# A state-space scan whose entering states are read into token rows and turned back by TensorE

## The reference

```
acum = jnp.cumsum(dtc * a_neg.reshape(ng, nr), axis=2)
decay = jnp.exp(jnp.where(mask, seg, -jnp.inf))
scores = jnp.einsum('bcign,bcjgn->bcijg', cc, bc)
y_intra = jnp.einsum('bcijgr,bcjgrp->bcigrp', scores[..., None] * decay, xdt)
...
y_inter = jnp.einsum('bcign,bcgrpn,bcigr->bcigrp', cc, s_prev, jnp.exp(acum))
y = (y_intra + y_inter)
```

## Time and profile before

| | us |
|---|---|
| median of 3 runs | 1627.63 |
| lowest and highest run | 1621.13, 1632.57 |
| span of the profiled execution | 1621.1 |
| TensorE busy in it | 1537.1 (95%) |
| DVE, ACT, POOL busy | 869.4, 795.1, 904.1 |

### The profile page before, as it was taken

How to read it: one execution, slowest core, us unless ns; L and a number is a source line. 1 busy time by engine, 2 the same in 40 slices (tenths; PEclk the granted TensorE clock), 3 DMA queues, 4 the chain that set the end, 5 groups by cost and what they waited for, 6 DMA issues and landing times.

```text
span 1621.1 us, 30898 instructions
## 1 busy us (share of the span) xinstructions
PE 1537.1 (95%) x11703; PEld 1460.5 (90%) x11703; DVE 869.4 (54%) x1806; ACT 795.1 (49%) x1450; POOL 904.1 (56%) x516
## 2 busy tenths in 40 slices
PE   4999998999999999999999999999989999999996
PEld 2899997887898999999899989789788989999996
DVE  0633202777436777712573449498873247777423
ACT  1655435767335544423676564565553345444333
POOL 0455555677572555557255556777753634555552
PEclk9999999999999999999999999999979999999998
DMA  8334346887551434434134323101213423344430
GB/s 334 103 117 127 121 129 215 289 302 264 188 163 53 125 121 129 145 130 155 52 93 157 105 92 104 41 27 41 40 52 133 143 91 105 129 130 128 136 125 39
DMA packets 57729, 209.63 MB, mean 129 GB/s; under 512 B 6288, under 2 KB 6416, under 8 KB 57232
## 3 DMA queue, kind: packets, MB, share of 16 engines
q1 hardware_dynamic: 56464, 205.96, 39.0%
q10 hardware_dynamic: 1152, 2.10, 0.4%
HBM read 200.63 MB, written 7.41 MB: 128 GB/s over the span
## 4 chain that ended last, share of the span: by engine, by line
PE 74%; issue 10%; DVE 8%; POOL 4%; ACT 3%; DMA 1%; POOLq 0%; DVEq 0%; SPq 0%; ACTq 0%
PE ps L755 6%; PE ps L757 6%; PE ps L756 6%; PE ps L663 6%; PE ps L665 6%; PE ps L664 6%; PE ps L998 4%; PE ps L999 4%; PE ps L1000 4%; PE ps L2737 3%; PE ps L2739 3%; PE ps L2738 3%; POOL wlo L318 3%; PE ps L388 2%; DVE ps L2311 2%
## 5 line engine op out<-in xcount | busy, mean ns | idle before, releaser
L318 POOL TENSOR_TENSOR wlo<-raw,whi 128x1024 fp32r<-128x1024 f32 (+1 forms) x195 | 494.1, 2535 | 445.7 <-ACT whi L306 445.4
L306 ACT ACTIVATE whi<-raw 128x1024 fp32r<-128x1024 f32 (+1 forms) x241 | 265.6, 1103 | 517.9 <-PE ps L665 187.5
L755 PE MATMUL ps<-hhi,whi 128*128 128x384 f32 x656 | 219.7, 335 | 2.5 <-POOL wlo L318 2.0
L829 DVE SCALAR_TENSOR_TENSOR evac<-ps,vec,evac 128x189 f32<-128x189 f32 (+3 forms) x440 | 167.4, 412 | 98.7 <-ACT evac L770 68.8
L757 PE MATMUL ps<-hhi,wlo 128*128 128x384 f32 x656 | 219.2, 334 | 0.0
L756 PE MATMUL ps<-hlo,whi 128*128 128x384 f32 x656 | 219.1, 334 | 0.0
L2502 POOL TENSOR_TENSOR wlo<-raw,whi 128x1024 fp32r<-128x1024 f32 x46 | 111.2, 2418 | 122.6 <-ACT whi L306 122.6
L998 PE MATMUL ps<-hhi,whi 128*128 128x384 f32 x392 | 133.3, 340 | 11.2 <-DVE hlo L450 10.6
L999 PE MATMUL ps<-hlo,whi 128*128 128x384 f32 x392 | 132.0, 337 | 0.0
L1000 PE MATMUL ps<-hhi,wlo 128*128 128x384 f32 x392 | 131.9, 337 | 0.0
L2737 PE MATMUL ps<-hhi,whi 128*128 128x384 f32 x368 | 126.5, 344 | 0.7 <-POOL wlo L2502 0.7
(11 more groups left out here) (352 smaller groups left out, 3511.2 us busy)
## 6 DMA issues: line engine op xcount, KB each, us to landing
raw<-w_in_in SPq DMA_DIRECT2D x98, 512.0 KB, 3.5
raw<-w_ada_in SPq DMA_DIRECT2D x96, 512.0 KB, 4.5
raw<-w_up_in SPq DMA_DIRECT2D x88, 512.0 KB, 3.5
raw<-w_down_in SPq DMA_DIRECT2D x32, 704.0 KB, 4.1
raw<-w_out_in SPq DMA_DIRECT2D x32, 512.0 KB, 3.5
qe<-e_keep SPq DMA_DIRECT2D x8, 512.0 KB, 7.0
s<-s_ssd_in SPq DMA_DIRECT2D x8, 256.0 KB, 4.4
o_ssd_out<-st_sb ACTq DMA_DIRECT2D x8, 256.0 KB, 2.2
```

Source lines behind the costliest of these rows:

```text
L306: act.activation(whi[:, z.mod(SPL), 0:p.kt * P], raw[:, b.mod(RAW), 0:p.kt * P], ACT.Copy).then_inc(hi_ready, 1)
L318: pool.tensor_tensor(wlo[:, z.mod(SPL), 0:p.kt * P], raw[:, b.mod(RAW), 0:p.kt * P], whi[:, z.mod(SPL), 0:p.kt * P].bitcast(F32), ALU.subt ...
L755: pe.matmul(out, a, hhi[:, k, :], start=(k == 0), stop=False)
```

## The change

The bank of the decays and its exponential go: `entry_decays` is deleted on TensorE and on ACT, with `e_in` and three semaphores. `entry(g, k)` takes C as the stationary operand and the states of the four heads as 256 moving columns, for each direction; its result has tokens on the partitions, so that a token's decay `exp(acum)`, which already lies in `dec_s` as a column for each head and direction, is a broadcast factor. `entered` on DVE becomes one multiply over 512 columns into `y_dir` and one addition of its two halves into `y_in`, now in token rows. The addition of L1451 in `gated_out` goes. In its place `outputs(u)` of the two latent chunks gets four further matmuls (two for each block `q`) with `y_in` stationary and the identity moving, which turn the rows back and accumulate in the outputs' bank; ahead of the first of them TensorE waits for `s_bw`, which `entered` raises.

```diff
-            def entry_decays(g, k):
-                act.wait_ge(s_eb, 2 * g + k + 1)
-                if g:
-                    act.wait_ge(s_bw, 2 * g - 1 + k)
-                act.activation(e_in[:, k].rearrange("p d n -> p (d n)"), ps[:, 4 + k, :], ACT.Exp).then_inc(s_ee, 1)
-
...
-                entry_decays(g, 0)
...
-                entry_decays(g, 1)
...
-            def entry_decays(g, k):
-                c = LAT1 + k
+            def entry(g, k):
+                b, c = g % 2, LAT1 + k
                 if k == 0:
                     pe.wait_ge(s_stout, g + 1)
-                else:
-                    pe.wait_ge(s_new, 2 * g + 2)
-                for d, m in enumerate(("le", "ge")):
-                    for h in range(4):
-                        n, r, col = (2 * d + h // 2) * P, 64 * (h % 2), 4 * g + 32 * d + h
-                        mm = pe.matmul(ps[r:r + 64, 4 + k, n:n + P], tok_s[:, 1, c, col:col + 1].to_broadcast([P, SSD_P]),
-                                       mask(m), tile_position=(0, r), start=True, stop=True)
-                mm.then_inc(s_eb, 1)
-
-            def entry(g, k):
-                b, c = g % 2, LAT1 + k
-                pe.wait_ge(s_ee, 2 * g + k + 1)
-                if k == 0:
                     pe.wait_ge(s_s0[b], 16 * (g // 2 + 1))
                     pe.wait_ge(s_new, 2 * g + 2)
                 for d, s in enumerate((s0, s1) if c == LAT1 else (s1, s0)):
-                    for q in range(2):
-                        mm = pe.matmul(ps[:, 4 + k, (2 * d + q) * P:(2 * d + q + 1) * P], s[:, b, d, q * P:(q + 1) * P],
-                                       proj[:, 24 + g, tokens(c)], start=True, stop=True)
+                    mm = pe.matmul(ps[:, 4 + k, d * 256:(d + 1) * 256], proj[:, 24 + g, tokens(c)], s[:, b, d, :],
+                                   start=True, stop=True)
                 mm.then_inc(s_in, 1)
...
                 for q in range(2):
...
-                                           start=(d == 0), stop=(d == 1))
+                                           start=(d == 0), stop=(c == CTX and d == 1))
+                    if c != CTX:
+                        if q == 0:
+                            pe.wait_ge(s_bw, 2 * g + c)
+                        for h in (2 * q, 2 * q + 1):
+                            r = 64 * (h % 2)
+                            mm = pe.matmul(ps[r:r + 64, 6 + u % 2, q * P:(q + 1) * P],
+                                           y_in[:, c - 1, h * SSD_P:(h + 1) * SSD_P], ident, tile_position=(0, r),
+                                           start=False, stop=True)
                 mm.then_inc(s_y, 1)
...
             def entered(g, k):
-                n = 2 * g + k
-                f, w = ps[:, 4 + k, 0:256], ps[:, 4 + k, 256:512]
+                n, c = 2 * g + k, LAT1 + k
+                dec = (dec_s[:, c, 0:64].rearrange("p (d h) -> p d h", d=2)[:, :, 4 * g:4 * g + 4]
+                       .unsqueeze(3).to_broadcast([P, 2, 4, SSD_P]))
                 dve.wait_ge(s_in, n + 1)
-                dve.tensor_tensor(w, w, e_in[:, k, 1, :], ALU.mult).then_inc(s_fw, 1)
-                dve.tensor_tensor(y_in[:, k, :], f, e_in[:, k, 0, :], ALU.mult).then_inc(s_fw, 1)
-                dve.wait_ge(s_fw, 2 * n + 2)
-                dve.tensor_tensor(y_in[:, k, :], y_in[:, k, :], w, ALU.add).then_inc(s_bw, 1)
+                dve.tensor_tensor(y_dir[:, k, :].rearrange("p (d h n) -> p d h n", d=2, h=4),
+                                  ps[:, 4 + k, :].rearrange("p (d h n) -> p d h n", d=2, h=4), dec, ALU.mult).then_inc(s_fw, 1)
+                dve.wait_ge(s_fw, n + 1)
+                dve.tensor_tensor(y_in[:, k, :], y_dir[:, k, 0:256], y_dir[:, k, 256:512], ALU.add).then_inc(s_bw, 1)
...
-                if c:
-                    dve.wait_ge(s_bw, 2 * g + c)
-                    dve.tensor_tensor(y, y, y_in[:, c - 1, :], ALU.add).then_inc(s_add, 1)
-                    dve.wait_ge(s_add, 2 * g + c)
```

More of the change, by code:

```diff
@@ L1068, in trunk @@
         xdt = tmp("xdt", [P, 2, 2, 256])
-        e_in = tmp("e_in", [P, 2, 2, 256])
+        y_dir = tmp("y_dir", [P, 2, 512])
         y_in = tmp("y_in", [P, 2, 256])
@@ L1074, in trunk @@
         s_out = [sem(f"s_out{k}") for k in range(2)]
[L1075 to L1078, removed]
+        (s_a, s_xtok, s_gm, s_r, s_seg, s_exp, s_ge, s_xw, s_st, s_dec, s_new, s_stout, s_xdt, s_y, s_in,
+         s_fw, s_bw, s_rlo, s_skip, s_v) = (sem(x) for x in (
+             "s_a s_xtok s_gm s_r s_seg s_exp s_ge s_xw s_st s_dec s_new s_stout s_xdt s_y s_in "
+             "s_fw s_bw s_rlo s_skip s_v").split())
         def tokens(c):
@@ L1337, in outputs @@
                 pe.wait_ge(s_xdt, u + 1)
+                g, c = u // 3, u % 3
                 for q in range(2):
```

## The result

| | us |
|---|---|
| before, median of 20 runs | 1628.15 (1621.13 to 1632.87) |
| after, median of 20 runs | 1632.26 (1625.09 to 1636.47) |
| ratio | 1.0028, 95% interval 1.0016 to 1.0039 |
| profiled execution after: span; with what lies around it | 1630.8; 1632.60 |

By the ratio the change makes the kernel 4.6 us slower (2.6 to 6.3); the two medians lie 4.1 us apart. That is inside 1%. The forecast was +6.6 us, 1634. Every run of after shows 1.8 us between its span and its time. The forecast had taken that as nothing; the later runs of before show the same 1.8 us, so it drops out of the difference.

The account below looks back on a forecast made before the run. TensorE, busy 95% of the span, was taken to bound the kernel. Its 0.93 us saving per group, set against waits for the rows, summed over groups to +6.6 us, so 1627.6 became 1634 us; range 1622 to 1643.

Parts of the forecast that it names:

- What leaves and joins TensorE: Per scan group: 1.95 us of entry_decays leave, 1.02 of turned rows join, entry unchanged; net 0.93 us saved, 7.4 in eight.
- The price on DVE: entered on DVE: product 687 ns, addition 0.42 us if nothing holds it; DVE saves about 0.5 us for a chunk.
- The wait for the rows in groups 3 to 6: In outputs(u+1) TensorE waits 2.4 us for DVE's addition, delayed by POOL's use of the SBUF ports.
- the second chunk: In outputs(u+2) TensorE waits only about 0.1 us for the rows, 0.5 where a group has 9 blocks.
- the forecast's softer reading: DVE's addition under POOL's L1219: both give way, so it merely runs slower, 0.66 us, ending at 338.53.
- Groups 1 and 2: TensorE waits about 0.9 us for the rows; group 1 changes by -0.4 us, group 2 by 0.
- The blocks' loads don't bind: Conditioning block loads in the scan: a longer group gives DMA more time, so they don't bind (share 0.80 to 0.85).
- The rival in which the rows are ready in time: entered(g, 0) done at 336.25 in group 3: 0.93 us kept per group, -7.4 us, 1620 us; chance 0.10.
- DVE ahead of POOL: Rival: L1464 starts before POOL's L1208, wait 1.1 us in groups 3 to 6, about 1629 us; chance 0.25.
- The clock falls: Rival: waits in groups 3 to 6 drop TensorE to 1.2 GHz, 1.7 us each; 1641 to 1644 us; chance 0.20.
- For group 7: Last group: waits of 0.2 and 0.9 us, 1.0 of turned rows, up to 0.9 back ahead of the DMA: +1.1 us.
- The sum: All eight scan groups: -0.6 - 0.4 + 0 + 1.56 + 3 x 1.64 + 1.1 = +6.6 us, giving 1634 us.

Follow-up runs that it names:

- a_late: The changed kernel with full loads and gates_lo(g-1) on DVE moved from ahead of entered(g, 0) to behind it; 1631.5 us, 1.0035 of before.
- a_short: The changed kernel with each conditioning block's load in the scan cut to its first quarter; 1628.8 us, 1.0013 of before.
- a_even: The changed kernel with full loads and the conditioning blocks of groups 1 to 6 spread two, one, one, three, one and the rest; 1.004 of before.
- a_short_late: The changed kernel with conditioning loads cut to a quarter and gates_lo(g-1) on DVE moved behind entered(g, 0); 1615.0 us, 0.9935 of before.
- b_short: The kernel before with each conditioning block's load in the scan cut to its first quarter; 1624.6 us, 0.999 of before.

## Why the prediction was right or wrong, point by point

- **What leaves and joins TensorE: right.** From the first turned row at 340.63 to the next work at 341.65 there are eight turned records and eight of L1321, 1.02 us, the 0.064 us a record that was forecast, and `entry` 0.97 us (336.04 to 337.01). Where next to nothing is waited for, groups are 18.2 to 18.3 us against 18.8 to 19.1: a net of 0.93 us forecast, 0.6 to 0.9 measured.
- **The price on DVE: right.** Product 0.68 us (0.69 forecast), addition 0.42 alone.
- **The wait for the rows in groups 3 to 6: right as a mechanism, hidden in the profile of after.** 2.4 us forecast, 2.15 measured once the loads were short; POOL's L1200 started 0.21 us ahead of L1446 (0.15 forecast), the third L1211 lay over the addition. At the second chunk 0.41 us were waited in groups 4 to 6 (0.5 forecast). The addition took 0.69 us; running at the slower pace gave 0.66 and waiting for L1211's end 0.75, so its length in group 3 doesn't tell these apart. Its end does: 340.58 is 0.28 us behind the end of the L1211 that ran when it started (340.30), and in group 7 it ended 0.29 us behind L318, after 2.52 us, where a slower pace would have given 0.66. The Trainium skill (SBUF — State Buffer, "SBUF: two separate sides") says that the first to start holds the shared ports for its whole instruction; with the 2.52 us the trace agrees, and the forecast's softer reading, in which both give way, doesn't fit the addition.
- **Groups 1 and 2: right with short loads** (waits of 0.75 us; 0.9 forecast), group 0 as well (0.25 us; 0.2 forecast).
- **"The blocks' loads don't bind": wrong.** This is the step that failed. I reasoned from the average, that a longer group gives DMA more time. What I left out is the time between the use of a slot and its next need: the deletion of two batches shortened the least of these from 5.7 to 4.0 us inside the group, while the time it gave back lay elsewhere. Waits for loads went from 2.5 to 12.6 us, and spreading the blocks took a part of that away again. It cost little against the forecast only because it took the place of the wait for the rows.
- **The rival in which the rows are ready in time (1620 us)** had a false condition. It said the 7.4 us are won if `entered` is done early enough. In a_late it was, and nothing was won; both had to go.
- **DVE ahead of POOL: did not happen** in after.
- **The clock falls: not in groups 3 to 6 of after**, where the wait for loads had broken the idle time into pieces of 0.25 to 0.8 us, nor in those groups of a_short, where four waits of 2.15 us stood whole at a granted clock of 1.00. But in group 5 of a_even it fell to 0.51 behind a wait of 2.19, so the rival was real: of the five waits for the rows of 2.1 to 2.2 us in groups 3 to 6 of these two profiles, one was followed by the lower clock. What sets it apart from the other four no run shows. In after it fell in group 7, behind idle times of 1.78 us (with 0.62 and 1.22 near it), and at the scan's end, behind 2.75, to 0.55 and 0.54, the 1.2 GHz level. For group 7 I had forecast +1.1 us; it went from 18.5 us (401.47 to 419.98) to 22.8 (410.17 to 432.93), +4.3. That term was mis-sized: it left out POOL's L318 over the addition, longer waits for loads (3.6 us, before 2.2), and the lower clock behind them.
- **The sum**: +6.6 forecast, +4.6 (2.6 to 6.3) measured. In the profiles it is 11.1 in the scan, 1.8 ahead of it and -3.3 behind, where the instructions are the same and the clock fell at other places; the medians say more of the size than this pair does. By groups 0 to 7 the forecast was -0.6, -0.4, 0, 1.6, 1.6, 1.6, 1.6 and 1.1; the profiles have -0.4, 0.0, 0.6, 1.5, 2.0, 1.6, 1.6 and 4.3. Groups 3, 5 and 6 are within 0.1 us of the forecast, but in after it was mostly loads that held them, and the wait for the rows would have given the same length alone (a_short). That one cause covered the other, and that the medians moved by less than the profiled scans did, is luck of the number; the wait of 2.15 us is not.

## What to carry to other kernels

When one engine starts to read what another engine makes, work out when it is ready, and then look for a second chain that ends at the same moment: taking either away shows nothing, and only both together show what the edit is worth (here 9.6 us by the medians of a_short_late and b_short). Deleting work from the bounding engine also shortens the time between the uses of a ring's slots; check the shortest distance between a use and the next need against the longest time from issue to landing, not the mean share of DMA alone.

## What the runs showed of the hardware that I had not expected

An addition of two SBUF operands on VectorE took 0.42 us alone. In after, a_short and a_short_late 20 of its 48 took longer, and each of these ended 0.28 to 0.29 us behind the end of the GpSimd instruction that was running when it started, whatever the length of that: 0.69 us under the last 0.41 us of an L1211, 1.12 under an L1201 of 1.9 us in a_short_late, 2.52 under an L318 of 2.3 us. Group 3 of a_short_late, DVE and then POOL:

```profile
335.03 1.12 DVE L1430 TENSOR_TENSOR y_in<-y_dir 128x256 f32<-128x256 f32 x1
```
```profile
333.98 1.89 POOL L1201 TENSOR_TENSOR seg_hi<-masks,tok_hi 128x1024 fp32r<-128x1024 f32 x1
```

The product with one PSUM operand took 0.68 to 0.69 us in all of its 16 places, with GpSimd at work or not. L1443 of the kernel before, an addition with one PSUM operand, took 0.42 us in all 16, also where a GpSimd instruction lay over the whole of it. So a result that another engine waits for is better added from PSUM; the changed kernel was not tried that way. And blocks of 512 KB took 3.3 to 7.3 us to land in the same 150 us, while those of 128 KB landed in 2.2 us (median); what was in flight beside them is a likely reason for the spread, not a shown one.
